# Two layers with a differential attention stage: another order of blocks, and VectorE's maximum ahead of the output in each step

## The reference

```python
def _diff_attend(q1, q2, k1, k2, v, lam):
    def blk(qs):
        a, b = qs
        s1 = jnp.einsum('bqhd,bkhd->bhqk', a, k1).astype(jnp.float32) * scale
        s2 = jnp.einsum('bqhd,bkhd->bhqk', b, k2).astype(jnp.float32) * scale
        w = jax.nn.softmax(s1, axis=-1) - lam * jax.nn.softmax(s2, axis=-1)
        return jnp.einsum('bhqk,bkhe->bqhe', w.astype(v.dtype), v)
    ...

def _diff_merge(o, subln_g, lam_init):
    return (_rms(o, subln_g) * (1.0 - lam_init)).reshape(o.shape[0], o.shape[1], -1)
```

## Time and profile before

| | |
|---|---|
| median of 3 runs | 3408.81 us (3407.46 to 3411.09) |
| the profiled execution: its time, its span | 3408.95 us, 3407.2 us |
| busy over the span: TensorE, VectorE, ScalarE, GpSimd | 94%, 49%, 36%, 21% |
| mean granted clock of TensorE | 0.979 |
| differential stage of layer 0, first maximum to last fin | 457.7 to 567.7 us |
| differential stage of layer 1, first maximum to last fin | 968.4 to 1049.6 us |

### The profile page before, as it was taken

One profiled execution on the slowest core, in us unless ns is written; L12 is line 12 of the kernel. 1 busy time (PEld: TensorE's weight loads), 2 busy tenths in 40 slices (PEclk: granted clock), 3 DMA queues, 4 the chain that ended last, 5 costly groups with the idle time before them and its releaser, 6 DMA issues.

```text
span 3407.2 us, 40024 instructions
## 1 busy us (share of the span) xinstructions
PE 3203.2 (94%) x16252; PEld 2527.6 (74%) x16252; DVE 1675.6 (49%) x2558; ACT 1212.0 (36%) x2068; POOL 715.3 (21%) x518
## 2 busy tenths in 40 slices
PE   6999988899988999989899999999999999999998
PEld 4777766677866788867788778887888776578886
DVE  2155555415764634457655553446444525564344
ACT  3242165434264322233344332224222325542222
POOL 3204312331513100046332300001000343230000
PEclk9999999999999999999899999999999999999999
DMA  5303210121102233222000133222232231022322
GB/s 225 118 20 115 88 41 24 49 97 47 56 28 78 81 93 105 88 89 93 19 7 1 50 103 108 93 93 87 87 105 87 81 111 38 1 87 93 107 86 80
DMA packets 77575, 260.55 MB, mean 76 GB/s; under 512 B 8400, under 2 KB 9552, under 8 KB 76240
## 3 DMA queue, kind: packets, MB, share of 16 engines
q1 hardware_dynamic: 76528, 253.28, 22.6%
q0 software_dynamic: 864, 4.72, 0.4%
HBM read 255.87 MB, written 2.10 MB: 76 GB/s over the span
## 4 chain that ended last, share of the span: by engine, by line
PE 86%; DVE 7%; ACT 4%; POOL 1%; issue 1%; DMA 1%; SPq 0%; ACTq 0%; DVEq 0%; POOLq 0%
PE banks L345 85%; PE banks L354 1%; POOL w_lo L336 1%; DVE area L576 1%; DVE x_lat L579 1%; DMA area<-in_w_mod 1%; DVE small L1778 0%; DVE area L1722 0%; DVE area L1760 0%; ACT area L434 0%; POOL w_late L336 0%; ACT area L437 0%; ACT w_hi L326 0%; POOL area L410 0%; DVE area L494 0%
## 5 line engine op out<-in xcount | busy, mean ns | idle before, releaser
L345 PE MATMUL banks<-area,w_hi 128*128 128x512 f32 (+4 forms) x5896 | 1770.5, 383 | 24.0 <-POOL w_lo L336 8.1
L345 PEld LDWEIGHTS banks<-area,w_hi 128*128 128x128 f32 (+2 forms) x5896 | 1078.8, 188 | 288.4 <-issue 24.2
L345 PE MATMUL banks<-area,w_lo 128*128 128x512 f32 (+4 forms) x2948 | 1120.2, 381 | 0.0
L345 PEld LDWEIGHTS banks<-area,w_lo 128*128 128x128 f32 (+2 forms) x2948 | 554.8, 188 | 119.1
L345 PE MATMUL banks<-area,w_late 128*128 128x512 f32 (+2 forms) x2316 | 579.1, 399 | 28.8 <-ACT area L532 14.8
L326 ACT ACTIVATE w_hi<-w_raw 128x1024 fp32r<-128x1024 f32 (+2 forms) x361 | 349.5, 971 | 544.9 <-PE banks L345 413.4
L345 PEld LDWEIGHTS banks<-area,w_late 128*128 128x128 f32 (+1 forms) x2316 | 434.6, 190 | 146.3 <-ACT area L532 18.1
L345 PE MATMUL banks<-area,area 128*128 128x64 f32 (+10 forms) x3896 | 468.6, 326 | 71.7 <-DMA area<-in_w_mod 17.5
L345 PEld LDWEIGHTS banks<-area,area 128*128 128x128 f32 (+4 forms) x3896 | 384.0, 183 | 157.7 <-issue 71.9
L410 POOL TENSOR_TENSOR area<-area,area 128x512 f32<-128x512 f32 (+1 forms) x102 | 139.6, 1371 | 1475.2 <-ACT area L395 1473.4
L336 POOL TENSOR_TENSOR w_lo<-w_raw,w_hi 128x1024 fp32r<-128x1024 f32 (+1 forms) x133 | 308.7, 2323 | 455.4 <-ACT w_hi L326 455.4
(11 more groups left out here) (236 smaller groups left out, 2274.6 us busy)
## 6 DMA issues: line engine op xcount, KB each, us to landing
w_raw<-in_l_ffn_w_in SPq DMA_DIRECT2D x176, 512.0 KB, 3.2
w_raw<-in_l_ffn_w_out SPq DMA_DIRECT2D x128, 384.0 KB, 3.1
w_raw<-in_w_in SPq DMA_DIRECT2D x66, 512.0 KB, 3.5
w_raw<-in_w_mod SPq DMA_DIRECT2D x32, 512.0 KB, 5.4
w_raw<-in_w_qkv SPq DMA_DIRECT2D x24, 512.0 KB, 3.2
w_raw<-in_l_w_in SPq DMA_DIRECT2D x22, 512.0 KB, 3.3
w_raw<-in_w_out SPq DMA_DIRECT2D x32, 320.0 KB, 2.9
area<-in_w_mod SPq DMA_DIRECT2D x8, 1024.0 KB, 16.6
```

The source lines that it names most:

```text
L345: return e.matmul(out, lhsT, rhs, start=first, stop=stop, skip_group_check=True)
```

## The change

Two edits in `LateStage`. The list of steps takes the blocks of a head in the order 0, 1, 4, 2, 3, 5 where the stage has six of them (layer 0); layer 1 keeps its order. And in VectorE's loop the maximum of step k comes first in its turn, ahead of o of step k-3 and fin of step k-4, in both layers. Nothing is added or left out.

```diff
@@ -1412,7 +1412,8 @@
                 self.h_end = place.at
-                self.steps = [(h_, i) for h_ in range(DF_HEADS) for i in range(total // P)]
+                blocks = (0, 1, 4, 2, 3, 5) if total == TA else range(total // P)
+                self.steps = [(h_, i) for h_ in range(DF_HEADS) for i in blocks]
                 self.n = len(self.steps)
...
@@ -1741,12 +1742,12 @@
                 for k in range(self.n + 4):
+                    if k < self.n:
+                        self.max_dve(q, e, k)
                     if 3 <= k < self.n + 3:
                         self.o_dve(q, e, k - 3)
                     if k >= 4:
                         self.fin_dve(q, e, k - 4)
-                    if k < self.n:
-                        self.max_dve(q, e, k)
                     if 1 <= k <= self.n:
                         self.combine_dve(q, e, k - 1)
```

## The result

The changed kernel takes 3428.62 us (median of 5 runs, 3417.02 to 3429.26) against 3407.95 (5 runs, 3407.1 to 3411.09): a ratio of 1.0049, 95% interval 1.0033 to 1.0064. That is slower by more than the 0.2% that can be told, and 17 us above the forecast of 3411.5. The profiled execution took 3428.62, its span is 3426.9 us, 19.7 more than before. The five runs aren't alike: three with a mean granted clock of 0.972 took 3428.62 to 3429.26, one with 0.975 took 3425.05, and one with 0.977 took 3417.02.

What follows compares the result with a forecast made beforehand. No engine was full; a circle of dependences through TensorE and VectorE set the pace. Layer 1 +2.8 and layer 0 -0.3 (-1.8 turns, -0.1 start, +1.6 drain) made +2.5 on 3408.95: 3411.5 us, range 3406.5 to 3417.

Steps and rivals of the forecast that it cites:

- The circle and the long turn: Dependence loop fin, transposes, scores, product, o: 4.61 us per long turn, 4.77 once the maximum ends last, 0.16 more.
- Layer 1: Sixteen long steps: 0.90 at the start, 0.16 at the next o and eleven turns of 0.16 more, together +2.8 us.
- In the drain behind the last maximum the order is as before: 0: Layer 1's end, after its last maximum: no change in time.
- The short turn: Layer 0's turn of short steps: VectorE's own work sets 2.65 us, the other paths being shorter.
- Six steps so cost 4 x 4.77 + 2 x 2.65: Layer 0's turns: 24.38 us per six steps against 24.56; fin(0) to fin(19) 75.8 against 77.6, -1.8.
- The start of layer 0: Step 2 now short saves 1.25 us at half clock, 1.15 given back: -0.1, bounds -1.2 to +1.0.
- The drain of layer 0: Step 22 now long, so two copies and a longer product lie in the open drain: +1.6 us.
- The third: Rival: maximum starts later behind its scores, in some 25 places; slower by more than 0.2%, 3420.5 us at 0.36 more; 9%.
- The second: Rival: maximum starts as the last score matmul leaves, o follows the product as before; 3408 us, within 0.2%; 13%.
- the first: Rival: VectorE's waits for the product in both layers close, gaining 23.9 us, 3385; 4%.
- the path of 2.44: Short turn of layer 0: path from fin through ScalarE's copy and short product to fin, 2.44 us, under 2.65.

Runs made afterwards that it cites:

- the filled kernel: Changed kernel plus unread matmuls in TensorE's waits at both stages' starts, in their drains and behind layer 0's short turns: 3406.02 us, ratio 0.9997 to the kernel before.
- the kernel before with filling: Kernel before plus unread matmuls ahead of the third scores and in the first two drain turns of both stages: 3398.19 us, ratio 0.9979.
- experiment 1: Against the kernel before, only the new order of blocks, the maximum staying behind fin: 3434.55 us, ratio 1.0077.
- experiments 3 and 4: Changed kernel plus unread matmuls: one behind short scores and four ahead of the next transposes, 3417.38 us; then only two ahead of the transposes, 3413.83 us.
- experiment 2: Against the kernel before, only the maximum moved first in both layers, blocks in the old order: 3423.93 us, ratio 1.0041.
- experiment 5: Against the kernel before, blocks 0, 1, 2, 4, 3, 5 and the maximum first in two turns of six, layer 0 only: 3409.83 us, ratio 1.0004.

## Why the prediction was wrong

Point by point, by its own steps:

- **The circle and the long turn: right.** 4.77 in all eleven turns of layer 1 and in the undisturbed ones of layer 0. The wait ahead of the maximum is 0.98 (0.97 foretold), and there is none ahead of o.
- **Layer 1: right in its parts, wrong in its drain.** fin(0) came +1.07 later (foretold 1.06), the eleven turns cost +1.8 (foretold 11 x 0.16). "In the drain behind the last maximum the order is as before: 0" was wrong: +2.6, since the clock is halved there, from 1055 for 6.8 us. At full clock, in the filled kernel, the same drain takes 16.5 where before took 16.7.
- **The short turn: right.** 2.63 to 2.65 against 2.65. The danger that I named for it, a late root of the next step, didn't show.
- **The step that failed: "Six steps so cost 4 x 4.77 + 2 x 2.65".** It prices a turn of long steps the same wherever it stands. Six of the twelve stand right behind a short one and took 6.23 to 6.29, +1.5 each, +8.9 together. So fin(0) to fin(19) was 84.65, not 75.8. A sum of durations from a stretch with the clock at 1.00 presumes that clock, and the earlier trace rows show both levels side by side in one stage. I used the 0.50 of 461 to 465 to price the start, and read it as a thing that happened there. I didn't ask what the new order leaves TensorE to do in 2.65 us: two transposes, four score matmuls, four product matmuls and a transpose back, busy 1.78 of the 2.63 us from fin to fin.
- **The start of layer 0: right**, -0.16 against -0.1. It holds at the half clock of that place only: with filling, at 1.00, fin(0) comes 0.69 later than in the kernel before with filling (13.83 against 13.14).
- **The drain of layer 0: the term of the sum was mis-sized.** +1.6 up to fin(21) was foretold. It was +4.6 (11.80 against 7.22). With the clock held the filled kernel takes 8.27, +1.05. The rest is the clock again: six transposes take 1.45 and the product of twelve 2.6, and with the waits between them this goes on for 17 us.
- **The rivals.** The third ended on the right side for a reason that didn't hold: the maximum doesn't lag more behind its scores at full clock, since the turns are 4.77. The second (4.61, nothing moves) and the first (the wait vanishes) are refuted by the same 4.77. None of the four had a clock that falls, and so none of their prices had it; of the bounds only that of layer 0's start had the clock in it, and the range ended at 3417.
- **A slip that decides nothing.** By its own figures the short product is 1.61 less 8 x 0.11, which is 0.73 and not 0.69; the path of 2.44 is then 2.48, still under 2.65.

In sum: +2.6 from the dependences, and some 17 more in the profiled execution. That the 2.6 is so close to the sum of 2.5 is luck in part: at a clock of 1.00 the turns are as foretold (-1.84 in layer 0, +1.83 in layer 1), but the start of layer 0 is +0.69, not -0.1, and its drain +1.04, not +1.6, and these two misses mostly cancel. Of the 17 the stages show 6 x 1.48 = 8.9 in turns, 4.5 in layer 0's drain (22.60 against 16.89 filled, less the 17.09 against 15.85 that the kernel before loses there itself) and 2.8 in layer 1's, less 0.9 at layer 0's start, where the kernel before loses more. The remaining 1.8 lie outside the stages, where executions differ by more (experiment 1's first maximum stands 5.3 earlier than that of the kernel before, with the same code ahead of it). The Trainium skill, TensorE: Matmul & The Clock Gate, section A second HAM failure mode: psum-queue depth-cycling, tells of a kernel in which short idle spells between groups of matmuls make the clock swing between its levels, at a cost in throughput. The trace agrees: behind each short turn, whose waits are 0.81 and 0.86, the clock is 0.50 for 3.4 us, and experiments 3 and 4 show the tie by filling the waits. It spoke against this change, and I didn't weigh it.

What stays open: the exact condition that makes the clock fall. The short turns of the kernel before, 3.4 to 4.0 long, didn't do it between 465 and 553; those of experiment 2, as long, did in some places and not in others; and in experiment 5 it fell in layer 1 where the code is that of before. No run here tells these apart.

## What to carry to other kernels

A schedule that makes one turn shorter can also make TensorE idle in it; list TensorE's work turn by turn for the new order, and where a turn has much less of it than its neighbours, work out the sum a second time with the next turn at half clock. Here that is 6.26 in place of 4.77, six times. Short steps next to each other, or spread through long ones, aren't equal even if their sums are. Before filling a wait of one engine, see whether the work put there was hidden already; and where TensorE must wait, a few matmuls that nobody reads, sized to the wait, can be worth more than another order: they alone took 0.1 to 0.2% off the kernel before.

## What the runs showed of the hardware

- The clock fell to half behind 3.5 us (498.50 to 502.00) in which TensorE was busy 2.13 and never waited longer than 0.86 at once. I had connected it with waits like the 5.48 of the earlier trace rows.
- Half clock costs much less than its length: 51 us more of it in the changed kernel (194 against 143), for some 17 us of time. What it costs differs by place: 1.48 us for the 3.4 of a turn behind a short one (six transposes take 1.45 in place of 0.77, but part of the turn is waiting), and 3.4 us for the 23 more that the changed kernel with filling has behind layer 1.
- A filling matmul of 128x128 by 256 columns in fp32 is two instructions of 0.216 each at full clock (1.73 us for eight).
- The kernel before, run again in sets of 21, 27 and 27 beside the experiments, ranged from 3399.94 to 3414.85, 0.4%; the spread goes with the mean granted clock (the three runs at 0.983 average 3400.3, the 33 at 0.979 average 3407.8, the three at 0.977 average 3412.8), though not closely (3407.36 to 3414.85 at 0.978). A difference of that size between two single executions therefore says little. Distances inside a stage say more where the clock is 1.00 in both: fin(0) to fin(11) of layer 1 is 50.67 to 50.69 in all seven kernels that keep the maximum behind fin there.
